# Eight rotation steps moved from behind the Fourier stage to beside the mixers' last wide products, and weight units split one piece later

## The reference

```
proj = rms_norm(x) @ w_in                     # 1024 x 3072, in 12 products of 256 columns
a_q, a_i, a_zf, a_zb, a_g, b_u, c_q, c_k, c_v = split(proj)
o_a = hgrn2_mixer(a_q, a_i, a_zf, a_zb, a_g)  # recurrence both ways, 4 heads of 64
o_b = fourier_mixer(b_u)                      # 2-D DFT over tokens and channels
q, k = rotary(c_q), rotary(c_k)               # t1 cos - t2 sin, t2 cos + t1 sin
o_c = dilated_window_attention(q, k, c_v)     # 8 heads of 64
x = x + concat(o_a, o_b, o_c) @ w_out
x = x + relu(rms_norm(x) @ w_up)**2 @ w_down
```

## Time and profile before

| | |
|---|---|
| median of 3 executions | 2459.89 us (2458.6 to 2463.41) |
| the profiled execution | 2462.22 us |
| its span | 2460.4 us |
| mean granted TensorE clock | 0.959 |
| TensorE busy | 2258.9 us, 92% |
| VectorE busy | 1314.1 us, 53% |
| ScalarE busy | 900.0 us, 37% |
| POOL busy | 213.9 us, 9% |

### The profile page before, as it was taken

The page is one execution under the profiler, slowest core; times in us unless marked ns, Lnnn a source line. Parts: engine busy times, 40 slices in busy tenths (PEclk is TensorE's granted clock), DMA queues, the critical chain, the costliest instruction groups (busy, mean ns, idle before and its releaser), DMA issues.

```text
span 2460.4 us, 33735 instructions
## 1 busy us (share of the span) xinstructions
PE 2258.9 (92%) x14488; PEld 1735.8 (71%) x14488; DVE 1314.1 (53%) x1931; ACT 900.0 (37%) x1329; POOL 213.9 (9%) x167
## 2 busy tenths in 40 slices
PE   6898799999999898799999998998899979899995
PEld 5777368888887785478888876565788548676673
DVE  6653655534436552746435455465433353677775
ACT  5332363212234322543222332244221123566663
POOL 1111200000010110210000020000000000222221
PEclk9899899999999999899999999999999988899997
DMA  4210102223222111012222221211111223689884
GB/s 154 69 52 35 52 28 93 101 88 103 98 90 86 52 52 52 18 59 96 98 91 103 95 81 54 94 61 53 69 62 54 87 86 148 230 329 356 342 326 195
DMA packets 51848, 270.21 MB, mean 110 GB/s; under 512 B 12144, under 2 KB 12272, under 8 KB 22512
## 3 DMA queue, kind: packets, MB, share of 16 engines
q1 hardware_dynamic: 41472, 256.67, 28.6%
q0 software_dynamic: 9216, 8.42, 1.0%
q10 hardware_dynamic: 1008, 2.92, 0.4%
HBM read 266.92 MB, written 26.21 MB: 119 GB/s over the span
## 4 chain that ended last, share of the span: by engine, by line
PE 82%; DVE 10%; ACT 5%; issue 1%; DMA 1%; POOL 1%; SPq 0%; DVEq 0%; ACTq 0%; POOLq 0%
PE psum L123 79%; PE psum L126 3%; DVE A_mix L136 2%; ACT A_mix L130 2%; DVE A_second L136 1%; DVE WL L136 1%; DVE A_second L144 1%; ACT WH L130 1%; DVE A_mix L156 1%; POOL A_mix L136 1%; ACT A_mix L133 0%; DMA raw<-in_w_in 0%; DVE A_moe L136 0%; DVE A_mix L162 0%; DVE A_mix L153 0%
## 5 line engine op out<-in xcount | busy, mean ns | idle before, releaser
L136 DVE TENSOR_TENSOR WL<-raw,WH 128x1024 fp32r<-128x1024 f32 x236 | 295.0, 1252 | 434.3 <-ACT WH L130 434.2
L130 ACT ACTIVATE WH<-raw 128x1024 fp32r<-128x1024 f32 x236 | 248.3, 1054 | 457.8 <-PE psum L123 437.4
L123 PE MATMUL psum<-HH,WH 128*128 128x512 f32 x736 | 307.6, 418 | 46.1 <-DVE A_second L136 20.8
L123 PE MATMUL psum<-R_op,WH 128*128 128x512 f32 x1024 | 316.2, 390 | 0.0
L123 PE MATMUL psum<-R_ffn,WH 128*128 128x512 f32 x1024 | 315.4, 389 | 0.0
L123 PE MATMUL psum<-HL,WH 128*128 128x512 f32 x736 | 294.5, 400 | 0.0
L123 PE MATMUL psum<-HH,WL 128*128 128x512 f32 x736 | 293.4, 399 | 0.0
L123 PE MATMUL psum<-A_mix 64*128 64x64 f32 (+5 forms) x1984 | 173.7, 320 | 59.5 <-DVE A_mix L136 38.8
L123 PEld LDWEIGHTS psum<-R_op,WH 128*128 128x128 f32 x1024 | 192.2, 188 | 40.8 <-issue 1.0
L123 PEld LDWEIGHTS psum<-R_ffn,WH 128*128 128x128 f32 x1024 | 192.2, 188 | 39.9
L123 PEld LDWEIGHTS psum<-HH,WH 128*128 128x128 f32 x736 | 142.6, 194 | 94.4 <-issue 32.1
(11 more groups left out here) (198 smaller groups left out, 2961.9 us busy)
## 6 DMA issues: line engine op xcount, KB each, us to landing
ring_moe<-in_w_gu SPq DMA_DIRECT2D x64, 1024.0 KB, 10.3
raw<-in_w_in SPq DMA_DIRECT2D x42, 1024.0 KB, 4.9
raw<-in_w_up SPq DMA_DIRECT2D x32, 1024.0 KB, 4.8
raw<-in_w_down SPq DMA_DIRECT2D x32, 1024.0 KB, 4.8
ring_moe<-in_w_dn SPq DMA_DIRECT2D x32, 1024.0 KB, 6.1
raw<-in_w_out SPq DMA_DIRECT2D x12, 1024.0 KB, 4.8
kept<-A_second SPq DMA_DIRECT2D x20, 256.0 KB, 2.1
raw<-in_dft SPq DMA_DIRECT2D x4, 1024.0 KB, 4.8
```

What stands on the lines that cost most here:

```text
L123: return self.raw.matmul(o, l, r, start=start, stop=stop)
L130: return self.raw.activation(o, i, f, scale=scale)
L136: return self.raw.tensor_tensor(o, a, b, op)
```

## The change

It has three parts.

1. **Rotation.** `rot_pe`, `rot_pool` and `rot_dve` become single steps for one tile i and are hung on the steps s15 to s22 of the tail (VectorE has one more, s23, because its addition for tile i - 1 stands behind its product for tile i). Step s15 lies behind the piece with index 31, s22 behind that with index 45. All eight matmuls use bank 7, one after the other, each waiting for VectorE's product of the one before. The factors are made at s14 (`rot_angles`). ScalarE's first Fourier copy waits for the last addition, since its target is the memory of the factors.
2. **Fourier stage and attention.** The second Fourier products go to banks 2 and 3. The scores start right behind them; the transposes of the first step wait for VectorE's last Fourier remainder (`free`).
3. **Late units.** `side_lins` gets a flag `late`: it then yields once before it finishes the product before and splits the unit, and once behind. It is set for the head and tail of both mixers and for the low-rank, shifted and gate products of the second block; not for the output products and the feed-forward part.

```diff
-        def side_lins(e, ls, made, split):
+        def side_lins(e, ls, made, split, late):
             before = None
             for l in ls:
                 for n in l.chunks:
                     for h in range(2):
+                        if late:
+                            yield
                         if before is not None:
                             made(e, before)
                             before = None
                         u = chunks[n][2] + h + 2
                         if u < len(units) and units[u][0] <= n + 1:
                             split(e, u)
                         yield
-                        yield
+                        if not late:
+                            yield
                 before = l
             made(e, before)
...
             for d in range(2):
-                e.wait_ge(*at("fou_act", ly, 0, d))
-                e.mm(bk(d), c("cd"), x.us[d], True, False)
                 e.wait_ge(*at("fou_act", ly, 1, d))
-                e.mm(bk(d), c("sd"), x.us[2 + d], False, True).then_inc(*did("fou_pe", ly, d))
+                e.mm(bk(2 + d), c("cd"), x.us[d], True, False)
+                e.mm(bk(2 + d), c("sd"), x.us[2 + d], False, True).then_inc(*did("fou_pe", ly, d))
...
+        ROT = 15
+
+        def turned_of(x, i):
+            return (x.cq3, x.ck3)[i // 4][:, i % 4, :], ("lin_act", "ps", x.tail[i // 2].n, i % 2)
+
+        def rot_pe(e, x, i):
+            src, made = turned_of(x, i)
+            e.wait_ge(*at(*made))
+            if i:
+                e.wait_ge(*at("rot_dve", x.ly, "s", i - 1))
+            else:
+                e.wait_ge(*at("nrm_dve", 2 * x.ly - 1, "col"))
+            e.mm(bk(7), c("rot64"), src).then_inc(*did("rot_pe", x.ly, i))
+
+        def rot_pool(e, x, i):
+            src, _ = turned_of(x, i)
+            e.wait_ge(*at("rot_pe", x.ly, i))
+            if i == 0:
+                e.wait_ge(*at("rot_dve", x.ly, "cos"))
+            e.tt(src, src, x.turn[0], MUL).then_inc(*did("rot_pool", x.ly, i))
...
+        def rot_dve(e, x, i):
+            if i < 8:
+                e.wait_ge(*at("rot_pe", x.ly, i))
+                e.wait_ge(*at("rot_dve", x.ly, "a", i - 2) if i >= 2 else at("rot_dve", x.ly, "sin"))
+                e.tt(x.rt[i % 2], bk(7), x.turn[1], MUL).then_inc(*did("rot_dve", x.ly, "s", i))
+            if i:
+                src, _ = turned_of(x, i - 1)
+                e.wait_ge(*at("rot_pool", x.ly, i - 1))
+                e.wait_ge(*at("rot_dve", x.ly, "s", i - 1))
+                e.tt(src, src, x.rt[(i - 1) % 2], ADD).then_inc(*did("rot_dve", x.ly, "a", i - 1))
...
             yield from between(pe_lins(e, x.head + x.tail), s0=lambda: pe_sum(e, 2 * x.ly - 1, x.before),
-                               s3=lambda: pe_column(e, 2 * x.ly - 1))
+                               s3=lambda: pe_column(e, 2 * x.ly - 1),
+                               **{f"s{ROT + i}": lambda i=i: rot_pe(e, x, i) for i in range(8)})
             yield from four_pe(e, x)
-            yield from rot_pe(e, x)
-            yield from att_pe(e, x.ly, scores, lambda h, k: x.cv3[:, k, h * 64:(h + 1) * 64], x, full, ready)
+            yield from att_pe(e, x.ly, scores, lambda h, k: x.cv3[:, k, h * 64:(h + 1) * 64], x, full, ready, free=free)
...
-            yield from between(act_lins(e, x.head + x.tail), **steps)
+            yield from between(act_lins(e, x.head + x.tail, True), **steps)
...
+            steps[f"s{ROT - 1}"] = lambda: rot_angles(e, x)
+            for i in range(9):
+                steps[f"s{ROT + i}"] = lambda i=i: rot_dve(e, x, i)
+            yield from between(dve_lins(e, x.head + x.tail, True), **steps)
             yield from four_dve(e, x)
-            yield from rot_dve(e, x)
...
-            wide = between(act_lins(e, s2.low + s2.shift), s0=lambda: act_twice(e), s1=positions,
+            wide = between(act_lins(e, s2.low + s2.shift, True), s0=lambda: act_twice(e), s1=positions,
...
-            weave(RWKV, c=rw_act(e), g=act_lins(e, s2.gates), b=iter(()))
+            weave(RWKV, c=rw_act(e), g=act_lins(e, s2.gates, True), b=iter(()))
```

More of the change, by code:

```diff
@@ L733, in side_lins, with act_lins, dve_lins @@
                         yield
-                        yield
+                        if not late:
+                            yield
                 before = l
             made(e, before)
[L738 to L742, removed]
+        def act_lins(e, ls, late=False):
+            yield from side_lins(e, ls, act_made, act_hi, late)
+        def dve_lins(e, ls, late=False):
+            yield from side_lins(e, ls, dve_made, dve_lo, late)
         def run(steps):
@@ L1194, in four_act @@
             for part in range(2):
+                if part == 0:
+                    e.wait_ge(*at("rot_dve", ly, "a", 7))
                 for d in range(2):
@@ L1208, in four_dve @@
                 e.wait_ge(*at("fou_act", x.ly, "hi", d))
-                e.tt(HLt[:, 2 + d, :], bk(d), HHt[:, 2 + d, :].bitcast(F32), SUB).then_inc(*did("fou_dve", x.ly, "lo", 2 + d))
+                e.tt(HLt[:, 2 + d, :], bk(2 + d), HHt[:, 2 + d, :].bitcast(F32), SUB).then_inc(*did("fou_dve", x.ly, "lo", 2 + d))
             yield
[L1212 to L1236, removed]
+        ROT = 15
+        def turned_of(x, i):
+            return (x.cq3, x.ck3)[i // 4][:, i % 4, :], ("lin_act", "ps", x.tail[i // 2].n, i % 2)
@@ L1237, in rot_dve, with rot_angles @@
+        def rot_angles(e, x):
             e.wait_ge(*at("tab_act", "cos64"))
             e.wait_ge(*at("tab_act", "sin64"))
[L1239 to L1254, removed]
+            e.wait_ge(*at("nrm_dve", 2 * x.ly - 1, "rs"))
+            e.tt(x.turn[0], TAB[:, 0:S], RS, MUL).then_inc(*did("rot_dve", x.ly, "cos"))
+            e.tt(x.turn[1], TAB[:, S:2 * S], RS, MUL).then_inc(*did("rot_dve", x.ly, "sin"))
@@ L1259, in build, with att_pe @@
         ATT = (0, 1, 2, 3, 7)
-        def att_pe(e, ly, scores, vtok, m, klen, ready, B=ATT):
+        def att_pe(e, ly, scores, vtok, m, klen, ready, B=ATT, free=None):
             def score(p):
@@ L1273, in turned @@
                 n = klen(p % 4) // 128
+                if p == 0 and free:
+                    free(e)
                 for hh in range(2):
@@ L1377, in win_act @@
                 sines = act_tables(e, 64, x.tab, 64)
-            yield from between(act_lins(e, x.head + x.tail), **steps)
+            yield from between(act_lins(e, x.head + x.tail, True), **steps)
             yield from four_act(e, x)
[L1380 to L1383, removed]
+            for i in range(2):
+                act_hi(e, chunks[x.out[0].chunks[0]][2] + i)
             yield from att_act(e, x.ly, x, full, evac)
@@ L1405, in win_pool @@
         def win_pool(e, x):
-            for _ in range(48 + 3):
-                yield
-            yield from rot_pool(e, x)
+            yield from between(range(48), **{f"s{ROT + i}": lambda i=i: rot_pool(e, x, i) for i in range(8)})
         MIX = "u" * 14 + "cuucu" * 12 + "c"
@@ L2837, in dve_program @@
             angles = dve_tables(e, 32, s2.tab, c("invf32"))
-            wide = between(dve_lins(e, s2.low + s2.shift), s0=lambda: dve_twice(e), s3=lambda: next(angles),
+            wide = between(dve_lins(e, s2.low + s2.shift, True), s0=lambda: dve_twice(e), s3=lambda: next(angles),
                            s5=lambda: next(angles), s13=lambda: scaled(0), s16=lambda: scaled(4))
             weave(LATENT, m=ml_dve(e), g=wide)
-            weave(RWKV, c=rw_dve(e), g=dve_lins(e, s2.gates), b=latent_dve(e))
+            weave(RWKV, c=rw_dve(e), g=dve_lins(e, s2.gates, True), b=latent_dve(e))
             mrg_dve(e)
```

5 lines of the change are left out of this document (3 added, 2 removed).

## The result

The changed kernel takes **2438.55 us** (median of 4 runs, 2433.16 to 2440.32), the kernel before 2460.36 in the same series (4 runs, 2458.6 to 2463.41). The ratio is 0.9906, 95% interval 0.9888 to 0.9925: 0.9% faster, by 21.8 us where the prediction has 34. So the result lies in the range, at the slow end of what was thought likely.

What follows compares the result with a forecast made beforehand. TensorE, busy 92% of the span, was taken as the bound. Two mixers at -21.4 us each (-42.8) plus +8.3 in the second block gave -34.5: 2427.7 from the profiled 2462.2, 2426 as median, range 2406 to 2449.

Steps and rivals of the forecast that it cites:

- rotation's stretch: Each mixer, between Fourier stage and first attention scores: moving the rotation away was to save 16.2 us per mixer.
- head's gap: TensorE's 7.02 us idle before a recurrence level at the mixer head's row product: was to fall to 1.5, -5.6 us.
- the one at 229: TensorE's 3.87 us gap at 229.01 in mixer 0: was to fall to 0.7, -3.2 us.
- latent rotation: Second block: VectorE's nine operations ahead of emptying a bank were to stall TensorE 5.7 us, +4.4 net.
- product starts: Second block's rwkv chains: five products with a step between their pieces start later, one by 1.5 us, +5.6 together.
- Seven of eight waits have a whole wide step behind them: Mixers' wide stretch: the argument that a full wide step or two hides VectorE's waits for all rotations but one.
- rotation's order: Mixers' wide stretch: VectorE waiting for each rotation delays recurrence levels, +1.3 us per mixer, bounds 0 and 11.
- rival A: Mixers: rotation waits push recurrence levels, up to 11 us per mixer, and the head's gap only half closes: 2453, chance 0.16.
- late units in the mixers: Mixers' wide products: units split behind their first piece were to save 14.0 us per mixer, half-clock relief included.
- Rival B: Both mixers: half-clock stretches behind TensorE's gaps vanish, 5 to 8 us more per mixer: 2412, chance 0.13.
- latent attention: Second block, attention steps after the latent rotation: VectorE runs ahead by a wide piece, -0.8 us, bounds -1 and +3.
- POOL beside VectorE: Mixers' rotation: POOL's products slow VectorE's additions by 0.3 us each, mostly off the path, +0.5 us per mixer.

Runs made afterwards that it cites:

- the split-only kernel: The changed kernel, but in the second block only the weight-unit split stands behind the first piece, with bank emptying ahead as before: 2418.88 us, ratio 0.9829.

## Why the prediction was right, and where it was off

**Right: sign, mechanism and the largest term.** The rotation's stretch is worth 16.15 us per mixer against 16.2, and no gap of TensorE there is ended by the transposes' new wait. The head's gap fell from 7.02 to 1.15 where 1.5 was forecast, the one at 229 from 3.87 to 1.25 where 0.7 was. The latent rotation stalls by 5.42 (5.7 forecast), though with 6.8 us at half clock at it and behind it where 3.4 was booked, and three product starts by 1.40 (1.5). The sum is -23.6 us in the traces against -34.5: the direction and most terms held, but the sum was 10.9 us too good, and the paragraphs below say where.

**"Seven of eight waits have a whole wide step behind them": false.** The prediction priced the rotation's order at 1.3 us per mixer; three gaps grew by 4.2 us together, where two had been given 1.3, and the rotation alone cost 2.8 more than the 8.8 booked for it in all. By `MIX`, and in TensorE's timeline, six of the eight rotations have a step of the recurrence right behind them and only those at 174 and 209 us (behind pieces 35 and 41) a wide piece. The level's differences and masked copies then queue on VectorE behind the product and the addition. I worked this out for rotation 1 (where the terms as listed add up to 6.4 and not 6.6) and took the others as covered without walking through VectorE's queue at each. Where a whole piece does follow each of the first seven, these gaps are back at their old size (-11 us). This is rival A's mechanism at a part of its size.

**The late units in the mixers were worth more**: 17.0 and 18.1 us against 14.0, because half clock left with the gaps (7.3 us of busy time in mixer 0, where 3.6 was booked). By the runs of each part alone the two errors cancel, 11.6 - 17.5 = -5.9 against 8.8 - 14.0 = -5.2, and that is luck. The parts don't simply add up either: made together they gave -1.6 and -5.2, because half clock came back at the rotation's gaps.

**The clock took 5 us back.** In the kernel after, the wide stretch of mixer 0 gains 3.6 us less than that of mixer 1, with the same gaps to 0.4 us, and its attention loses 1.7, the price of 3.4 us at half clock at 324. Behind the gap of 7.3 us both mixers have the same stretch, here mixer 0's:

```profile
269.60:279.80 10.20, 6.30 (x18) 2.90 (x20) 6.87 (x22) 5.50 (x13) 0.00 (x0) 0.50 0.30 104
```

Rival B wanted it gone; the gap keeps it.

**The step that failed is the latent attention's.** Booked at -0.8 ("VectorE runs ahead by a whole wide piece"; bounds -1 and +3), it cost 5.5, outside these bounds. The prediction did not count what hangs on the wide stream there: six operations of the emptying, a remainder (1.22) and four scalings of X (2.73) ahead of the row minimum of 1608.49, 3.87 us for TensorE and 3.4 us of half clock behind it. With the emptying ahead of the piece this is gone, which is shown by the split-only kernel. It is 6.3 of the 10.9 us by which the sum was off.

**POOL beside VectorE.** I took 0.3 us for a collision from one addition of 0.96, booked 0.5 per mixer and set the page's rule aside. That addition was issued when POOL's product had 0.4 us left. The same trace had one that was issued just behind the start of a POOL product, which I passed over (VectorE, then POOL):

```profile
274.92 1.74 DVE L136 TENSOR_TENSOR A_mix<-A_mix 128x512 f32<-128x512 f32 x1 [0.56 <-POOL A_mix L136]
```

```profile
274.85 1.26 POOL L136 TENSOR_TENSOR A_mix<-A_mix 128x512 f32<-128x512 f32 x1
```

In the kernel after the additions beside POOL take 1.16 to 2.29, and a remainder takes 2.16 while a POOL product runs until 194.19 (VectorE, then POOL):

```profile
193.11 2.16 DVE L136 TENSOR_TENSOR WL<-raw,WH 128x1024 fp32r<-128x1024 f32 x1 [2.89 <-ACT WH L130]
```

```profile
192.93 1.27 POOL L136 TENSOR_TENSOR A_mix<-A_mix 128x512 f32<-128x512 f32 x1 [3.25 <-PE psum L123]
```

The remainder ends 1.08 us after POOL, and alone it takes 1.22, so it did next to nothing before POOL was done. The product with one operand from PSUM takes 687 ns beside POOL and 689 without. The Trainium skill, page "SBUF — State Buffer", section "SBUF: two separate sides", says that the lock concerns a VectorE operation with two SBUF inputs only against a GpSimd operation that reads SBUF. The trace agrees on both sides of that condition: 917 against 773 ns with two SBUF inputs, 687 against 689 with one. I had cited the rule without it. Held were, by the estimate above, 5.9 us per mixer, between the 2.4 of my row (8 x 0.3) and the 10 of the rule taken whole, and the time shows little of it.

## What to carry to other kernels

Two actions that sit in one step of an ordered queue rarely want the same place: here the split of a unit gained some 34 us by moving behind a piece (ratio 0.9963 without it, 0.9824 with it alone), and the emptying of a bank, moved along in the second block, lost 19 (0.9906 against 0.9829). Move each alone and ask of each what is queued behind it. A cross-engine helper (matmul, product, addition) belongs in front of a long piece of the busy engine, not in front of the step that this engine reaches next. And price two parts together, not each alone: the rotation gave 7.0 us by itself and 1.1 beside the late units, because its gaps brought half clock back.

## What was not expected of the hardware

- POOL lengthened VectorE's operations only where both their operands are in SBUF: 917 against 773 ns and 1492 against 1222 ns, but 687 against 689 with one operand from PSUM.
- The same instructions behind the same gap of 3.96 us are followed by 3.4 us at 1.2 GHz in one execution and by 6.8 us in another; behind a gap of 1.7 us by none or by 6.8.
- At each of the three longer gaps in mixer 0 (at 150, 166 and 200) or just behind it half clock began, 3.4, 6.8 and 6.8 us of it; the last 6.8 us stood there before the change too, behind a gap of 1.69. As 1.2 GHz is half of 2.4, 6.8 us of it cost up to 3.4 (an estimate), so a gap of 2.1 us could cost 5.5 in all. The one at 167:

```profile
167.20:174.00 6.80, 6.80 (x33) 5.72 (x32) 4.71 (x5) 2.00 (x2) 1.27 (x1) 0.50 0.00 0
```
